# Cached keys of eight sampled rows: sixteen gather-and-attend steps taken two at a time, with six buffers of gathered rows in place of five

## The chip, the cores and the metric

The kernel runs on one core of a Trainium2 chip. The metric is the time of one execution on the device in microseconds (us). The engines are named as the profile names them: PE (matmul, with PEld for its weight loads), DVE, ACT, POOL and SP. DMAs are issued by SP or ACT, and, where the rows to fetch are looked up in a list of indices, by POOL.

## What is computed

One layer of a hybrid decoder for a prompt of 1024 rows and for eight sampled rows that each look back on 4096 cached rows. Only the sampled rows' attention over the cache is touched by the change:

```python
lat_past = cache_lat[page_table].reshape(Bd, -1, MLA_KV_RANK)      # 8 x 4096 x 128, gathered by pages
kr_past = cache_kr[page_table].reshape(Bd, -1, MLA_ROPE)           # 8 x 4096 x 32
q_lat = jnp.einsum('bshn,rhn->bshr', q_nope, w_uk)
s_past = jnp.einsum('bshr,btr->bhst', q_lat, lat_past) + jnp.einsum('bshp,btp->bhst', q_rope, kr_past)
s = jnp.concatenate([s_past, s_new], axis=-1) * MLA_SCALE
p = jax.nn.softmax(s, axis=-1)
o_lat = jnp.einsum('bhst,btr->bshr', p, lat_all)
```

Ahead of it stand the modulation, the input projection, the gated linear attention and the prompt's own attention; behind it the output projection and the layer norm of all rows.

## The kernel before

Each engine has its own program, written out by hand, and semaphores order them. The prompt's attention ends at about 560 us of the span. Then PE works through the cache in NSTEPS = 16 steps, two for each of the eight sampled rows. Step n handles 2048 cached rows: 128 partitions with 16 cached rows each, which is 128 x 2048 latent values and 128 x 512 rotary ones (1.3 MB).

For a step, PE does four things, and the rest of this text uses these letters for them:

- T(n): `keys_transposed(n, j)` for j = 0 to 3 (16 transposes of 128 x 128, L2403, into banks 0 to 3) and `rotary_transposed(n)` (4 more, L2410, bank 4). ACT copies each bank out (`keys_out`, L1267 and L1269). The key banks are single: a transpose of step n+1 into bank j waits until ACT has copied step n's bank j.
- S(n): `scores(n)`, 16 products over the latent keys (L2452) and 4 over the rotary ones (L2455), each f32 product being two instructions. They use 32 columns of the array each, so that four run beside each other.
- wT(n): `weights_transposed(n)`, one 128 x 128 transpose of the softmax weights (L2462).
- W(n): `weighted(n)`, 16 products with 32 columns each (L2471) that read the gathered rows themselves.

Between S and wT stand DVE's maximum (`largest`, L1758) and ACT's exponential (`weights`, L1277); between wT and W stands DVE's copy (`weights_out`, L1764); after W comes DVE's copy of the result (`values_out`, L1770). PE's order in loop round n is T(n+2), wT(n), S(n+1), W(n). ACT's is the five copies of step n+2, then the exponential of step n+1.

POOL issues the gathers (`gather(n)`, L872, L874, L875). There are UNITS = 5 buffers, and step n uses buffer n mod 5. A gather is two indirect DMAs, latent rows (L874) and rotary rows (L875). Buffer 2 lies in two pieces (slabs 1 and 2 of z), so its latent rows come in two DMAs (L872) and a gather into it is three. The first three gathers (2, 0, 1) are issued while the prompt's attention still runs; 3 and 4 wait for its last product; from 5 on, gather n waits for W(n-5) and for the maximum of step n-4.

The last two rounds carry extra work: PE's matmuls that spread the layer's gate over all rows (`gates_of_prompt`, `gates_of_samples`, L2476 and L2479), ACT's split of the output weights into a high part (`high_out`, L1281), eight pieces that go into buffers as they come free, and POOL's and ACT's split of the first prompt rows. Then DVE and PE merge the sixteen partial results (L1781 to L1807) between the first matmuls of the output projection (`high_rows`, L2495 and L2496). The gathered rows of steps whose buffers are slabs 1 and 2 and of the last ones must be read before ACT writes output weights over them.

## Time and profile before

| | us |
|---|---|
| runs shown (median of 3) | 745.33 |
| lowest, highest | 743.96, 746.56 |
| the profiled execution | 743.97 |
| its span in the trace | 742.1 |
| granted TensorE clock, mean | 0.995 of full |
| stretch from the first T in the loop to the first output matmul | 562.71 to 638.29 |

The span is the time from the first recorded instruction to the last; 1.9 us of the execution lie around it. A timeline row gives start, duration, engine, line, operation, output and input, shape, the count of merged instructions, and in brackets how long the engine was idle before it and what is taken to have ended the wait ("issue" means that the profile shows nothing that it waited for). Rows of PEld are the weight loads, and for f32 products they follow each other as the array takes them, so the start of one group to the start of the next is what the group costs PE. PE's own durations have the depth of the pipeline in them.

### The profile page before, as it was taken

How to read it: one execution, taken by the hardware profiler on the slowest of the kernel's cores; microseconds unless marked ns; L12 is line 12 of the kernel's file. 1: busy time of each engine (PE TensorE's matmuls, PEld its weight loads, DVE VectorE, ACT ScalarE, POOL GpSimd, SP SyncE). 2: the span in 40 equal slices, each digit the busy share in tenths (PEclk: the TensorE clock that was granted, in tenths of full speed). 3: DMA queues.
4: the chain of work that ended last, by engine and by line, in shares of the span. 5: the costliest groups of instructions: out<-in, count | busy, mean ns of one | idle time of the engine just before them, and what ended most of it. 6: DMA issues, size and time to landing. Idle time of an engine off the chain costs nothing.

```text
span 742.1 us, 16684 instructions
## 1 busy us (share of the span) xinstructions
PE 705.5 (95%) x7025; PEld 546.4 (74%) x7025; DVE 355.3 (48%) x782; ACT 327.3 (44%) x779; POOL 75.6 (10%) x113
## 2 busy tenths in 40 slices
PE   2799999999999999999999999999999999999995
PEld 1486878788789986777766666777677889678884
DVE  0454380030202025777675576667671111389977
ACT  1254651121212137667656566645675667602100
POOL 0000000000000010101111201132113443000000
PEclk9999999999999999999999999999999999999999
DMA  9995300303001011000010000202756774103332
GB/s 293 396 375 174 114 0 1 114 0 97 0 1 57 1 43 51 9 14 11 10 11 1 1 1 1 59 1 76 240 183 222 274 267 175 60 1 116 123 132 85
DMA packets 35301, 70.31 MB, mean 95 GB/s; under 512 B 6626, under 2 KB 17979, under 8 KB 33564
## 3 DMA queue, kind: packets, MB, share of 16 engines
q1 hardware_dynamic: 30602, 47.73, 19.8%
q0 software_dynamic: 4016, 20.97, 8.1%
q8 instruction: 56, 0.92, 0.5%
q10 hardware_dynamic: 610, 0.55, 0.3%
q14 instruction: 17, 0.14, 0.1%
HBM read 62.26 MB, written 6.07 MB: 92 GB/s over the span
## 4 chain that ended last, share of the span: by engine, by line
PE 90%; DVE 3%; SPq 2%; DMA 2%; ACT 1%; issue 1%; another core or an unknown queue 1%; DVEq 0%; ACTq 0%
PE banks L1988 21%; PE banks L2174 8%; PE banks L2000 6%; PE banks L2302 5%; PE banks L2383 4%; PE banks L2403 3%; PE banks L2152 3%; PE banks L2512 3%; PE banks L2514 3%; PE banks L2513 2%; PE banks L2090 2%; PE banks L2009 2%; PE banks L2452 2%; PE banks L2471 2%; PE banks L2495 2%; DMA s_x<-in_x_prompt 2%
## 5 line engine op out<-in xcount | busy, mean ns | idle before, releaser
L1044 ACT ACTIVATE s_z<-banks 128x512 f32<-128x512 f32 (+3 forms) x40 | 19.6, 501 | 130.0 <-PE banks L1988 130.0
L1988 PE MATMUL banks<-s_w_parts,s_h_b 128*128 128x272 f32 (+3 forms) x328 | 68.0, 323 | 0.0
L1253 ACT ACTIVATE s_z<-banks 128x512 f32<-128x512 f32 (+2 forms) x88 | 41.4, 517 | 47.1 <-PE banks L2383 46.3
L1417 DVE COPY s_zs<-banks 8x512 f32<-8x512 f32 (+3 forms) x6 | 3.5, 576 | 118.5 <-PE banks L1962 118.5
L1988 PEld LDWEIGHTS banks<-s_w_parts,s_h_b 128*128 128x128 f32 x328 | 49.3, 189 | 4.9 <-issue 1.7
L1244 ACT ACTIVATE s_z<-banks,s_temps 128x896 f32<-128x896 f32 (+7 forms) x64 | 47.2, 742 | 11.6 <-DVE s_temps L1712 8.6
L1988 PE MATMUL banks<-s_w_parts,s_h_a 128*128 128x256 f32 (+2 forms) x256 | 49.7, 314 | 0.0
L1988 PE MATMUL banks<-s_z_r,s_h_b 128*128 128x512 f32 (+1 forms) x152 | 48.8, 387 | 0.0
L2383 PEld LDWEIGHTS banks<-s_ident,s_z 128*128 128x128 f32 x288 | 33.3, 141 | 11.8 <-issue 5.5
L2383 PE MATMUL banks<-s_ident,s_z 128*128 128x128 f32 x288 | 39.8, 274 | 1.6 <-DVE s_z L1728 1.6
L1988 PE MATMUL banks<-s_z_r,s_h_a 128*128 128x512 f32 x128 | 40.9, 395 | 0.0
L1988 PEld LDWEIGHTS banks<-s_w_parts,s_h_a 128*128 128x128 f32 x256 | 36.0, 189 | 3.6 <-issue 0.4
L2302 PE MATMUL banks<-s_z 128*64 128x128 f32 x576 | 38.5, 278 | 0.0
L1267 ACT ACTIVATE s_z<-banks 128x512 f32<-128x512 f32 x64 | 33.1, 602 | 9.3 <-PE banks L2403 7.6
L2302 PEld LDWEIGHTS banks<-s_z 128*64 128x64 f32 x576 | 30.8, 136 | 5.4 <-issue 5.4
L1350 ACT ACTIVATE s_temps<-s_temps,s_eps_t 128x1 f32<-128x1 f32 (+1 forms) x9 | 2.6, 294 | 72.2 <-DVE s_temps L1845 72.2
L1728 DVE TENSOR_SCALAR s_z<-s_z,s_temps 128x896 f32<-128x896 f32 (+7 forms) x64 | 33.2, 540 | 1.7
L1712 DVE TENSOR_REDUCE s_temps<-banks 128x1 f32<-128x896 f32 (+3 forms) x32 | 32.8, 1024 | 1.1
L1988 PEld LDWEIGHTS banks<-s_z_r,s_h_b 128*128 128x128 f32 x152 | 28.5, 188 | 5.6
L1988 PEld LDWEIGHTS banks<-s_z_r,s_h_a 128*128 128x128 f32 x128 | 24.0, 188 | 6.7 <-issue 0.8
L2174 PE MATMUL banks<-s_kt,s_temps 96*128 96x512 f32 (+1 forms) x64 | 25.9, 527 | 0.0
L2174 PE MATMUL banks<-s_kt,s_z 96*128 96x512 f32 (+2 forms) x64 | 25.2, 515 | 0.0
(391 smaller groups left out, 1520.7 us busy)
## 6 DMA issues: line engine op xcount, KB each, us to landing
s_z<-in_w_ada SPq DMA_DIRECT2D x16, 512.0 KB, 12.2
s_temps<-in_w_in SPq DMA_DIRECT2D x3, 2048.0 KB, 7.7
s_x<-in_x_prompt SPq DMA_DIRECT2D x8, 512.0 KB, 11.8
s_z<-in_w_ada SPq DMA_DIRECT2D x1, 4096.0 KB, 13.8
s_kt<-in_w_out SPq DMA_DIRECT2D x8, 512.0 KB
s_temps<-in_x_prompt SPq DMA_DIRECT2D x8, 512.0 KB
out_y_prompt<-s_temps SPq DMA_DIRECT2D x7, 512.0 KB
s_temps<-in_w_in SPq DMA_DIRECT2D x2, 832.0 KB, 14.2
```

Source lines behind the costliest of these rows:

```text
L1244: last = nc.scalar.activation(weights_of(s, u), score_of(s, u), ACT.Exp, bias=nmx[:, c:c + 1], accum_out=rsum[:, c:c + 1])
L1253: nc.scalar.activation(PTb[r % 3][:, 4 * g:4 * g + n, :], banks[:, 4 + (groups(r) + g) % 2, 0:P * n].rearrange("p (j q) -> p j q", j=n), A ...
L1267: nc.scalar.activation(latT(n, j), banks[:, j, :], ACT.Copy).then_inc(f_Tc, 1)
L1712: nc.vector.tensor_reduce(nmx[:, c:c + 1], score_of(s, 0), AX_X, ALU.max, negate=True).then_inc(mx_ready, 1)
L1728: last = nc.vector.tensor_scalar(weights_of(s, u), weights_of(s, u), rinv[:, c + u:c + u + 1], None, ALU.mult)
L1988: last = nc.tensor.matmul(banks[:, proj_bank(c, t), 0:WIDTH[c]], h_[half][:, k, n0:n0 + P], w_, start=(k == 0 and n == 0), stop=(k == KT - ...
L2000: last = nc.tensor.matmul(banks[:, proj_bank(1, u), :], w_[:, k, P * m:P * m + P], h_[half][:, k, :], start=(k == 0 and n == 0), stop=(k = ...
L2152: last = nc.tensor.matmul(banks[:, q_bank(n, q), 0:384], z[:, BLOCKS[n], P * k:P * k + P], w_uq[:, k, 384 * q:384 * q + 384], start=(k == ...
L2174: last = nc.tensor.matmul(score_of(s, u)[:, n0:n1], QTb[n % 4][:, h, :], KTh[:, h, n0:n1], start=True, stop=True)
L2302: last = nc.tensor.matmul(banks[64 * par:64 * par + 64, 6, 0:P], V(j, 2 * hp + par), block, start=(j == 0), stop=(j == i))
L2383: last = nc.tensor.transpose(banks[:, 4 + k0 % 2, P * (b % 4):P * (b % 4) + P], Pm[r % 3][:, P * b:P * b + P], ident[:])
L2403: last = nc.tensor.transpose(banks[:, j, P * r:P * r + P], cached(n, 4 * j + r), ident[:])
```

## The change

- PE's loop goes over n = 0, 2, ..., 12 and does T(n+2), T(n+3), wT(n), wT(n+1), S(n+2), W(n), W(n+1), S(n+3). S(1) comes before the loop, next to S(0). The last two steps' wT and W stand behind the loop among the gate matmuls, all of which come after the last S.
- The scores of odd steps get a place of their own (bank 6, columns 256 to 383); both turned weights of a pair lie in bank 6; both results of a pair lie in bank 7, and DVE copies them out at once (128 x 256).
- ACT copies out ten banks (steps n and n+1) and then makes the weights of n and of n+1. DVE copies the two weights, then takes the maximum of n+2, copies the two results, and takes the maximum of n+3.
- wT(n) waits until the weights of both n and n+1 are there; W(n) of even n waits for DVE's copy of the last pair.
- Six buffers: the new one, buffer 3, is made of two query buffers of the prompt's attention (`qt1`, `qt3`, widened from 96 to 128 partitions). Buffers 2 and 3 are now the ones in two pieces, with three DMAs for a gather. Gather 3 is issued once the last scores of the prompt are done. Gathers 4 and 5 wait for the prompt's last product. From 6 on, gather n waits for W(n-6), and no longer for a maximum.
- ACT's high parts of the output weights go into the buffers in another order; the first is made before the weights of step 15 and all others after them. POOL's split waits for T(14).

```diff
-UNITS = 5
+UNITS = 6
+IN_HALVES = (2, 3)
...
-        w_out_hi = [slab_r(EARLY_SLABS[0]), slab_r(EARLY_SLABS[1]), slab_r(FIRST_KEYS[0]), slab_r(FIRST_KEYS[1]),
-                    z_rf[:, LAT3:LAT3 + D], z_rf[:, LAT3 + D:LAT3 + LAT], z_rf[:, LAT4:LAT4 + D], z_rf[:, LAT4 + D:LAT4 + LAT]]
+        w_out_hi = [z_rf[:, LAT3:LAT3 + D], z_rf[:, LAT3 + D:LAT3 + LAT], z_rf[:, LAT4:LAT4 + D], z_rf[:, LAT4 + D:LAT4 + LAT],
+                    slab_r(FIRST_KEYS[0]), slab_r(FIRST_KEYS[1]), slab_r(EARLY_SLABS[0]), slab_r(EARLY_SLABS[1])]
...
+        def scores_of(n):
+
+            return banks[:, 5, 0:P] if n % 2 == 0 else banks[:, 6, 256:256 + P]
...
+            pool.wait_ge(sc_done, len(STEPS))
+            gather(3)
             pool.wait_ge(pv_done, N_PAIRS_OF_HEADS)
-            for n in range(3, UNITS):
+            for n in range(4, UNITS):
                 gather(n)
             for n in range(UNITS, NSTEPS):
                 pool.wait_ge(f_o, n - UNITS + 1)
-                pool.wait_ge(f_mx, n - 3)
                 gather(n)
...
-            weights(0)
-            for n in range(NSTEPS):
-                if n + 2 < NSTEPS:
-                    for j in range(5):
-                        keys_out(n + 2, j)
-                if n + 1 < NSTEPS:
-                    weights(n + 1)
...
+            for n in range(2):
+                weights(n)
+            for n in range(2, NSTEPS, 2):
+                for j in range(5):
+                    keys_out(n, j)
+                for j in range(5):
+                    keys_out(n + 1, j)
+                weights(n)
+                if n == NSTEPS - 2:
+                    high_mixed(0)
                     act.wait_ge(w_out_in, 16 * KT)
...
+                    high_out(0)
+                weights(n + 1)
+            act.wait_ge(f_o, 12)
+            for k in range(1, 4):
+                high_out(k)
...
-            for n in range(NSTEPS):
+            for b in range(NB):
+                n = HALVES * b
                 weights_out(n)
-                if n + 1 < NSTEPS:
-                    largest(n + 1)
-                if n + 1 == NSTEPS:
+                weights_out(n + 1)
+                if b + 1 < NB:
+                    largest(n + 2)
+                else:
                     dve.wait_ge(f_mx, NSTEPS)
                     nc.vector.tensor_reduce(nmin, nm, AX_X, ALU.min).then_inc(f_dm, 1)
-                values_out(n)
+                values_out(b)
+                if b + 1 < NB:
+                    largest(n + 3)
...
             def weights_transposed(n):
-                pe.wait_ge(f_p, n + 1)
-                if n >= 1:
-                    pe.wait_ge(f_pTc, n)
-                nc.tensor.transpose(banks[:, 6, 0:P], p_s[n % 2], ident[:]).then_inc(f_pT, 1)
+                if n % 2 == 0:
+                    pe.wait_ge(f_p, n + 2)
+                    if n >= 2:
+                        pe.wait_ge(f_pTc, n)
+                nc.tensor.transpose(banks[:, 6, P * (n % 2):P * (n % 2) + P], p_s[n % 2], ident[:]).then_inc(f_pT, 1)
...
             scores(0)
-            for n in range(NSTEPS):
-                if n + 2 < NSTEPS:
-                    all_transposed(n + 2)
...
-                weights_transposed(n)
-                if n + 1 < NSTEPS:
-                    scores(n + 1)
...
-                weighted(n)
+            scores(1)
+            for n in range(0, NSTEPS - 2, 2):
+                all_transposed(n + 2)
+                all_transposed(n + 3)
+                weights_transposed(n)
+                weights_transposed(n + 1)
+                scores(n + 2)
+                weighted(n)
+                weighted(n + 1)
+                scores(n + 3)
+            pe.wait_ge(p_tabs, 16)
+            pe.wait_ge(f_Tc, 5 * NSTEPS)
+            gates_of_prompt(0)
+            gates_of_samples(0)
+            gates_of_prompt(1).then_inc(gate_b, 1)
+            weights_transposed(NSTEPS - 2)
+            weights_transposed(NSTEPS - 1)
+            gates_of_samples(1).then_inc(gate_b, 1)
+            pe.wait_ge(f_dm, MERGE["min"])
+            nc.tensor.transpose(banks[0:NB, 6, 256:256 + P], nmin, ident[:]).then_inc(p_pe, 1)
+            weighted(NSTEPS - 2)
+            weighted(NSTEPS - 1)
```

## Rows read from the trace of the kernel before

**Rows 1.** The page: busy time by engine, and the chain that ended last.

```profile
PE 705.5 (95%) x7025; PEld 546.4 (74%) x7025; DVE 355.3 (48%) x782; ACT 327.3 (44%) x779; POOL 75.6 (10%) x113
...
PE 90%; DVE 3%; SPq 2%; DMA 2%; ACT 1%; issue 1%; another core or an unknown queue 1%; DVEq 0%; ACTq 0%
```

**Rows 2.** Timeline of PEld, one round of the loop (n = 2).

```profile
573.51 1.73 PEld L2403 LDWEIGHTS banks<-s_ident,s_z 128*128 128x128 f32 x16 [0.20 <-issue]
575.21 0.47 PEld L2410 LDWEIGHTS banks<-s_ident,s_z 128*128 128x128 f32 x4
575.65 0.14 PEld L2462 LDWEIGHTS banks<-s_ident,s_z 128*128 128x128 f32 x1
575.95 0.81 PEld L2452 LDWEIGHTS banks<-s_z,s_temps 128*32 128x32 f32 x32 [0.17 <-issue]
...
576.96 0.89 PEld L2471 LDWEIGHTS banks<-s_z 128*32 128x32 f32 x32
578.06 0.20 PEld L2403 LDWEIGHTS banks<-s_ident,s_temps 128*128 128x128 f32 x2 [0.20 <-issue]
```

**Rows 3.** Timeline before the loop: 64-column products (L2302) between 128-column transposes.

```profile
552.63 0.42 PEld L2302 LDWEIGHTS banks<-s_z 128*64 128x64 f32 x8 [0.17 <-issue]
553.22 0.86 PEld L2383 LDWEIGHTS banks<-s_ident,s_z 128*128 128x128 f32 x8 [0.17 <-DVE s_z L1728]
554.05 0.91 PEld L2403 LDWEIGHTS banks<-s_ident,s_temps 128*128 128x128 f32 x8
```

**Rows 4.** Timeline of the first round: PEld, DVE and ACT.

```profile
562.27 0.24 PEld L2455 LDWEIGHTS banks<-s_z,s_temps 128*32 128x32 f32 x8
...
565.55 0.42 PEld L2410 LDWEIGHTS banks<-s_ident,s_w_uq 128*128 128x128 f32 x4 [0.85 <-issue]
...
565.77 0.29 DVE L1758 TENSOR_REDUCE s_temps<-banks 128x1 f32<-128x128 f32 x1 [5.81 <-remote]
...
568.97 0.14 PEld L2403 LDWEIGHTS banks<-s_ident,s_z 128*128 128x128 f32 x1 [0.20 <-issue]
```

**Rows 5.** Timeline of PEld, the round n = 3.

```profile
582.63 0.14 PEld L2455 LDWEIGHTS banks<-s_z,s_temps 128*32 128x32 f32 x2 [1.11 <-issue]
...
583.84 0.14 PEld L2403 LDWEIGHTS banks<-s_ident,s_temps 128*128 128x128 f32 x1 [0.20 <-issue]
```

**Rows 6.** Timeline of POOL: gather 2, gathers 3 and 4, gather 6, gather 7.

```profile
513.30 0.95 POOL L875 DMA_INDIRECT s_w_uq<-in_cache_k_rope,s_idx  x1 [0.30 <-issue]
...
559.91 0.95 POOL L874 DMA_INDIRECT s_z<-in_cache_kv_latent,s_idx  x1 [13.98 <-PE banks L2302]
...
563.66 0.95 POOL L875 DMA_INDIRECT s_z<-in_cache_k_rope,s_idx  x1 [0.30 <-issue]
...
573.89 0.94 POOL L874 DMA_INDIRECT s_temps<-in_cache_kv_latent,s_idx  x1 [2.35 <-PE banks L2471]
...
578.43 0.94 POOL L872 DMA_INDIRECT s_z<-in_cache_kv_latent,s_idx_half  x1 [2.35 <-PE banks L2471]
...
580.92 0.95 POOL L875 DMA_INDIRECT s_w_uq<-in_cache_k_rope,s_idx  x1 [0.30 <-issue]
```

**Rows 7.** Timeline of ACT: weights of step 3, first copies of step 5.

```profile
577.65 0.37 ACT L1277 ACTIVATE s_z<-banks,s_temps 128x128 f32<-128x128 f32 x1 [0.89 <-DVE s_temps L1758]
...
578.75 1.09 ACT L1267 ACTIVATE s_z<-banks 128x512 f32<-128x512 f32 x2 [0.65 <-PE banks L2403]
```

**Rows 8.** Stretches of 1 us: busy and count by engine, clock, DMA share, GB/s.

```profile
579.00:580.00 1.00, 1.00 (x12) 1.00 (x11) 0.00 (x0) 1.00 (x3) 0.70 (x2) 1.00 0.38 152
...
585.00:586.00 1.00, 1.00 (x12) 1.00 (x11) 0.00 (x0) 1.00 (x4) 0.69 (x2) 1.00 0.36 78
```

**Rows 9.** Timeline of PEld, behind the last full round.

```profile
630.53 0.30 PEld L2476 LDWEIGHTS banks<-s_modB,s_z 128*128 128x128 f32 x2 [0.20 <-issue]
...
634.78 0.22 PEld L2479 LDWEIGHTS banks<-s_modB,s_z 128*32 128x32 f32 x2
...
638.29 0.19 PEld L2495 LDWEIGHTS banks<-s_z_r,s_front_parts 128*128 128x128 f32 x1 [0.20 <-issue]
```

More of the change, by code:

```diff
@@ L281, in hybrid_step @@
         taken[0] = MLA_AT
[L282 to L283 removed]
+        qt1, qt3 = sb("qt1", [P, H * P]), sb("qt3", [P, H * P])
+        QTb = [v.rearrange("p (h s) -> p h s", h=H) for v in
+               (z[0:QK, 2, W_GV:W_GV + H * P], qt1[0:QK], carve(H * P, rows=QK), qt3[0:QK])]
         nmx = carve(8)
@@ L1276, in weights @@
                 b, c = divmod(n, HALVES)
-                nc.scalar.activation(p_s[n % 2], banks[:, 5, 0:P], ACT.Exp, bias=nm[:, b, c:c + 1],
+                nc.scalar.activation(p_s[n % 2], scores_of(n), ACT.Exp, bias=nm[:, b, c:c + 1],
                                      accum_out=o_all[:, b, c, KVR:KVR + 1]).then_inc(f_p, 1)
@@ L2470, in weighted @@
                         window = pTx[n % 2][:, g, :, :].rearrange("p r q -> p (r q)")[:, 32 * r:32 * r + 32]
-                        last = nc.tensor.matmul(banks[32 * g:32 * g + 32, 7, 0:KVR], window,
+                        last = nc.tensor.matmul(banks[32 * g:32 * g + 32, 7, KVR * (n % HALVES):KVR * (n % HALVES) + KVR], window,
                                                 cached(n, 4 * g + r), start=(r == 0), stop=(r == 3))
```

83 lines of the change are left out of this document (33 added, 50 removed).

## The prediction

> **What bounds the kernel now.** I read the page first. PE is busy 95% of the span and makes 90% of the chain that ended last [rows 1], so what counts is PE's own stream in the stretch that the change touches. That stretch is 562.71 to 638.29, 75.6 us. Next I read PEld's timeline, because the start of one group to the start of the next is what a group costs PE.
>
> One round takes 578.06 - 573.51 = 4.55 us [rows 2]. It divides into T 2.14 (573.51 to 575.65), wT 0.30, S 1.01 and W 1.10. The only idle times in it are 0.17 ahead of S and 0.20 ahead of the next T. Nobody releases them ("issue"), and they stand where the shape goes from 128*128 to 128*32 and back. Between wT and the T ahead of it, both 128*128, there is none; nor is there one between S and W, both 128*32, though W waits for two semaphores. Before the loop the same 0.17 stands ahead of 64-column products and behind them, and not between two kinds of 128-column transposes [rows 3]. I take the gap as the price of changing the shape of the weight tile.
>
> Three of the rounds are longer. The first takes 568.97 - 562.71 = 6.26: DVE gets its first scores at 565.77, three us after PE loaded the last weights of S(0), and PE itself is idle in pieces, the longest 0.85 [rows 4]. The round n = 3 takes 5.78, with a pause of 1.11 in the midst of S(4) [rows 5], and n = 8 repeats both. The other rounds from 1 to 13 take 4.55 each. POOL's rows show what is common: these two rounds hold the gathers into buffer 2, three DMAs in place of two, and the first round has four DMAs in one go, 559.91 to 564.61 [rows 6]. PE's pause ends 0.76 after the third issue ends (581.87), and each such round is longer by 1.24, which is one issue with its gap (0.94 + 0.30). I call this a hold. Its cause isn't in the trace. Gather 2, three DMAs ending at 514.25, met other PE work and no hold, so three issues alone don't make one [rows 6].
>
> **The change part by part.** The sum is made against the profiled execution, 743.97, which lies 1.36 under the median of the three runs, 745.33.
>
> *Order of PE's loop.* Nothing is removed from PE's work; two changes of shape in every two rounds go. A pair costs two T at 2.14 (4.28), the first wT 0.11 and the second 0.30, S 1.01, and W twice without its gap (1.10 - 0.22 = 0.88 each). The second S has ten turns of four matmuls at 0.11, thus 1.09, for it doesn't start on an empty array, and then 0.22 for the change back. Together 8.77 against 9.10 [rows 2]. Seven pairs save 7 x 0.33 = 2.3 us. Bounds: nothing, if the gap belongs to a wait after all, and 7 x 0.37 = 2.6.
>
> *Cover of ACT and DVE.* In the round before, ACT's weights begin 1.70 after S began (575.95 to 577.65) and its first copy 0.69 after T began [rows 2, 7]. In a pair the weights of n+1 end some 0.95 after T(n+2) began, so the ten copies start 0.26 later than a copy could. ACT makes a copy every 0.5 (two in 1.09), so bank 3 is free 3.0 after the pair began and bank 4, whose copy is a little longer, at 3.5; T(n+3) wants them at 3.45 and 3.84. It holds by 0.3. The copies of n+3 end at 6.1, S(n+3) wants them at 7.4. wT(n) now waits for two exponentials, the second of which is made at the start of the same pair, 3.3 early; behind it S and both W would queue. W(n) waits for DVE's copy, ready 5.1 after the pair began and wanted at 5.7. Cost 0; without that cover it would be 0.3 to 0.6 a pair.
>
> *Start.* S(1) ahead of the loop waits for ACT's copies of step 1, about 0.3. If the hold of f_sc stays until 565.7 [rows 4], ACT is the next to be late: it makes both first weights, to 567.2, before it copies T(2) out, and T(3) needs those banks. Copy by copy T(3) ends at 570.5, and the second pair begins at 574.9. Before, the third round began at 573.51, and with S(3) added 574.6. So this pair loses 0.3 where the sum above has it gain 0.33: +0.6. Bounds: 0 without the hold, +0.9.
>
> *Gathers.* The maximum that POOL waited for is long past before and goes without effect. From W(n)'s end to the start of pair n+4 are 10.4 us, for the second gather of a pair two more. POOL issues a pair of gathers in 4 or 6 DMAs of 1.24, thus 5.0 or 7.5, in a pair of 8.8, so it isn't the bound. A gather's data are through some 6 us after its first issue (573.89 to about 580), one of three DMAs after 7 to 8 (578.43 to about 586) [rows 6, 8]. For the pair 8 and 9 (and 14 and 15) the second is issued 3.7 after the first and is through at 11.7 against 12.6 allowed: free, by 0.9. Bounds: 0 and, if DMAs of both queue up, 1 to 2 us each.
>
> The Trainium skill ("DMA: Bandwidth & Descriptors", Bandwidth) would have transfers of at least 1 MiB and so speaks against pieces: by its fit (Anatomy of one DMA) a half costs an estimated 2.0 + 1.2 us, and six DMAs one after another about 18 us, which would make both pairs late by 5. The trace doesn't agree that the fixed parts add up: three DMAs were through after 8 us where this gives 9, and the DMA share falls to 0.36 only once all three are through.
>
> *Holds.* Before, two rounds pay 1.24. After, gathers 8, 9, 14 and 15 have three DMAs, but they go out as two runs of six, and all other gathers as runs of four. Part of each run falls on transposes. The fifth and sixth issue of a run of six end as S(n+4) begins, which is where the holds stood. I take two holds of 1.24, as before: 0. Bounds: -2.5 (none) and 1.7 to 2.5 for each of five runs, which is the excess of the first round and twice 1.24. Gather 3, moved ahead to 549.5, has three issues over 64-column products: between 0 (gather 2) and 1.24; I take 0, the row with the same three DMAs. On POOL nothing urgent is queued behind gather 3, and gathers 4 and 5 leave when 3 and 4 did.
>
> *End.* Before, 638.29 - 630.53 = 7.76 with S(15) in it, 6.7 without [rows 9]. After, the same matmuls stand there in another order, with two changes of shape fewer (0.4) but the minimum's transpose waits for both of DVE's copies behind wT(15), with only one gate matmul over them (0.4): 0, between -0.4 and +0.4. ACT's high parts end at 7.9 behind the last S and the merge wants ACT at 8.4, so this hides too; if it didn't, up to 1 us. DVE's copy of the last results is twice as wide and adds 0.1 to the merge. POOL's split of the first prompt rows stands behind its last gather, issued a pair and more before, and waits only for ACT.
>
> Sum: -2.3 + 0.3 + 0.6 + 0 + 0 + 0.1 = -1.3; with the start's wait for ACT's copies under the hold, -1.5. This gives 742.5 for the profiled execution and 743.8 from the median.
>
> **The rivals.**
>
> *The holds go away.* They stood where S met the third issue. If the new places (transposes under the third and fourth issue) have none, 2.5 more is gained, and if the first round's goes too, its excess of 1.7: 739.6 to 741.3, say 740.5. For it: gather 2. Against: the first round's reached into T(2) [rows 4].
>
> *A hold with every run of issues (slower than before).* All gathers go out in runs of four or six, and the only run of four before, at the start, cost 1.7 [rows 4, 6]. Three runs of four at 1.7 and two of six at 2.5, less the two old ones, is +7.6: 751.4. It decides from 0.3 us extra in each of the five runs on.
>
> *A late second gather or a late bank.* The margins are 0.9 for gathers 9 and 15 and 0.3 for ACT's copies. One or two of them missed cost 1 to 3: 745.3 to 747.
>
> *The change doesn't do what it says.* If the 0.17 and 0.20 belong to something in each step, the 2.3 stay away: about 746.
>
> **How the numbers follow.** A measurement of this kernel can tell about 0.3%, 2.2 us, from no change. Chances: my forecast (741.8 to 745.8 by its own bounds) 0.42, of which 0.15 gains over 2.2; holds gone 0.22, all faster; holds everywhere 0.14, all slower; late gather or bank 0.12, of which 0.09 slower; no effect 0.10, of which 0.02 slower. Faster 0.37, same 0.38, slower 0.25. The range reaches from the case with all holds gone, 739.5, to 748.5, in which a late gather and small holds are; the full price of holds everywhere stays out (0.14), and a little on the other side.
>
> **What will show it.** Right: pairs of 8.8 us in PEld's timeline, with one gap of 0.17 and one of 0.20 in each; "DMA" or ACT as releaser of T(9) or T(15) would show the third rival. A pause with "issue" inside S or T after the third or later indirect DMA shows holds; their number and place decide between the first two rivals. My start is right if DVE's first maximum comes near 565.7 and T(3) goes at ACT's pace. Wrong would be everything here if gaps of 0.17 stood inside W or between W and S.

## The result, and the profile after

The kernel after takes 771.0 us (median; 767.07 to 774.57), the kernel before beside it 745.9: ratio 1.034, interval 1.028 to 1.039. The forecast was 743.8 in a range of 739.5 to 748.5; range and sign were wrong.

The page of the kernel after: busy time, PE's busy share and TensorE's granted clock in 40 slices, and the chain that ended last.

```profile
PE 720.5 (94%) x7025; PEld 554.6 (72%) x7025; DVE 353.2 (46%) x774; ACT 326.1 (42%) x779; POOL 78.3 (10%) x116
...
PE   2799999999999989999999999999988788999996
...
PEclk9999999999999999999999999899999998999998
...
PE 90%; DVE 3%; issue 3%; ACT 1%; DMA 1%; ACTq 1%; another core or an unknown queue 0%; DVEq 0%
```

Busy times and chain look like [rows 1]. What points at the fault is small: "issue" at 3% in place of 1%, digits 8 and 7 in PE's row over the loop where the page before has 9 throughout, and three digits 8 in the clock. The same marks in both traces find it. From the start to the rotary DMA of gather 2 the profiled execution after is 3.71 longer (513.30 and 517.01), from there to the last transposes of step 1 another 1.66, over the scores ahead of the loop 3.77 (S(0) alone took 1.23, S(0) and S(1) take 5.00; some 1.1 of it is S(1), which the loop no longer has), from the first T of the loop to the first output matmul 18.57 (75.58 and 94.15), behind it -0.05. The sum is 27.66 = 771.63 - 743.97.

Stretches of the loop after: T(2) and T(3); S(2), W(0), W(1); S(3); then T(4) and T(5); later T(6) and T(7); T(12) and T(13); last a whole pair without gathers. Columns: stretch, its length, PE busy (operations), granted clock, DMA share, GB/s.

```profile
571.85:576.27 4.42, 4.42 (x41) 1.00 0.51 208
576.58:579.45 2.87, 2.87 (x106) 1.00 0.00 0
579.45:583.27 3.82, 2.52 (x48) 1.00 0.67 217
583.27:589.59 6.32, 6.12 (x41) 0.73 0.70 287
...
596.58:605.45 8.87, 6.79 (x40) 0.81 0.58 219
...
637.56:646.45 8.89, 7.48 (x41) 0.62 0.59 213
...
650.83:659.63 8.80, 8.80 (x190) 1.00 0.01 4
```

A pair that no gather disturbs takes 8.80 us; the forecast had 8.77. With a run of gathers, S of the odd step takes 3.8 to 4.0 in place of 1.21, and the transposes behind it 5.2 to 8.9 in place of 4.42. In three of these stretches TensorE's granted clock is below full (1.00 is 2.4 GHz, 0.50 is 1.2), behind the pauses of PE; (1 - clock) x length is 1.7, 1.7 and 3.4 us.

The timeline of one hold, after: POOL, PEld, DVE and ACT.

```profile
579.06 0.94 POOL L884 DMA_INDIRECT s_temps<-in_cache_kv_latent,s_idx  x1 [9.09 <-PE banks L2489]
580.30 0.95 POOL L885 DMA_INDIRECT s_temps<-in_cache_k_rope,s_idx  x1 [0.30 <-issue]
580.36 0.16 PEld L2469 LDWEIGHTS banks<-s_z,s_temps 128*32 128x32 f32 x5 [0.35 <-issue]
581.08 0.17 PEld L2469 LDWEIGHTS banks<-s_z,s_temps 128*32 128x32 f32 x5 [0.56 <-issue]
...
581.81 0.18 PEld L2472 LDWEIGHTS banks<-s_z,s_temps 128*32 128x32 f32 x5 [0.55 <-issue]
...
583.26 0.85 PEld L2418 LDWEIGHTS banks<-s_ident,s_z 128*128 128x128 f32 x6 [0.59 <-issue]
...
584.94 0.29 DVE L1768 TENSOR_REDUCE s_temps<-banks 128x1 f32<-128x128 f32 x1 [3.39 <-remote]
585.27 0.37 ACT L1288 ACTIVATE s_z<-banks,s_temps 128x128 f32<-128x128 f32 x1 [6.54 <-DVE s_temps L1768]
```

Two things start with the run of issues. PE stops when the first issue ends (580.00) and then gets through five or six weight loads and their products every 0.73 us, where an undisturbed S makes 40 weight loads in 1.1. And DVE's largest of step 3, whose scores end at 582.97, starts 1.97 later; ACT's exponential waits for it, and ACT's copies of T(4), which T(5) needs, stand behind the exponential. In this kernel that chain costs PE little: ahead of T(5) and its like PE stands 0 to 0.3 us, 0.7 in the five pairs together. The rest is PE's own slow pace and the clock: of the 12.7 us too much in the transposes 10.9 are in the first twenty of each pair (2.13 when undisturbed), where PE gets through four every 1.43 us while a run of six goes on:

```profile
597.99 0.42 PEld L2418 LDWEIGHTS banks<-s_ident,s_temps 128*128 128x128 f32 x4 [0.90 <-issue]
599.42 0.42 PEld L2418 LDWEIGHTS banks<-s_ident,s_temps 128*128 128x128 f32 x4 [1.01 <-issue]
```

Pauses of the first kind I call slow supply, late starts of the second kind late wake. Both stand in all five pairs with gathers. In the run of six, DVE's largest starts 4.76 after its scores end.

### The profile page after: what moved, and what is told of

Its sections match the earlier page's. It is cut to its first block, busy times and chain, and to the rows that moved or that the text cites. A ratio compares the mean times of both kernels' runs of the same rounds, so it can differ in the third digit from the quotient of the medians.

```text
span 769.8 us, 16643 instructions
## 1 busy us (share of the span) xinstructions
PE 720.5 (94%) x7025; PEld 554.6 (72%) x7025; DVE 353.2 (46%) x774; ACT 326.1 (42%) x779; POOL 78.3 (10%) x116
## 4 chain that ended last, share of the span: by engine, by line
PE 90%; DVE 3%; issue 3%; ACT 1%; DMA 1%; ACTq 1%; another core or an unknown queue 0%; DVEq 0%
PE banks L2003 20%; PE banks L2189 8%; PE banks L2015 6%; PE banks L2317 4%; PE banks L2418 4%; PE banks L2398 4%; PE banks L2167 3%; PE banks L2469 2%; PE banks L2530 2%; PE banks L2532 2%; PE banks L2531 2%; PE banks L2105 2%; PE banks L2024 2%; PE banks L2489 2%; PE banks L2513 2%
## 5 line engine op out<-in xcount | busy, mean ns | idle before, releaser
L1288 ACT ACTIVATE s_z<-banks,s_temps 128x128 f32<-128x128 f32 x16 | 5.9, 367 | 49.2 <-DVE s_temps L1768 49.0
```

## The experiments

In each group the kernels ran on one chip beside the kernel before. The span and the clock of every run come from a recorded execution; so nothing here tells what a run without recording would do. Edits are shown in part; "..." marks what is left out.

### On a chip where the kernel before takes 746.5 us

**a_no_gathers.** The loop of gathers n = 6 to 15 is left out, and PE's transposes wait only for a buffer's first gather.

```
-            for n in range(UNITS, NSTEPS):
-                pool.wait_ge(f_o, n - UNITS + 1)
-                gather(n)
...
-                pe.wait_ge(f_in[n % UNITS], (48 if n % UNITS in IN_HALVES else 32) * (n // UNITS + 1))
+                pe.wait_ge(f_in[n % UNITS], (48 if n % UNITS in IN_HALVES else 32))
```

> Changed kernel without the gathers of steps 6 to 15 (24 indirect DMAs of POOL); the last ten steps read the rows of steps 0 to 5 again, so the sample part of the output is not the reference's. Every theory has the holds come from these gathers, so the pairs should all take about 8.8 us like the two that have none running (T(14) at 650.83 to the gates at 659.63 in the changed kernel). The loop then lasts 7 x 8.8 = 61.6 us; in the changed kernel the stretch from T(2) (571.85) to the gates (659.63) is 87.8, so 26 us go: 771.0 - 26 = 745, and no fall of the granted clock inside the loop. If the pairs stay at 12 us or more, the gathers are not the cause and all three theories fall.

743.5 us, ratio 0.995 (0.994 to 0.997); two pairs of it, columns as above:

```profile
579.39:588.20 8.81, 8.81 (x191) 1.00 0.01 2
588.20:597.00 8.80, 8.80 (x191) 1.00 0.02 4
```

From the first T of the loop to the first output matmul it takes 67.99. The gathers of the loop thus cost 94.15 - 67.99 = 26.2 us in the kernel after: 13.5 in the five S of odd steps (over 1.21 each) and 12.7 in the five stretches of transposes behind them (over 4.42 each).

**a_small.** All 24 issues of the loop stay, with 128 bytes a row.

```
+                for out in outs + [kro[n % UNITS]]:
+                    nc.gpsimd.indirect_dma_start(out[:, 0:ROPE], None, one_rows, at).then_inc(f_in[n % UNITS], 16)
...
-                gather(n)
+                gather_small(n)
```

> Changed kernel in which every one of the 24 indirect DMAs of steps 6 to 15 is still issued by POOL at its place, over 128 rows, but moves 128 bytes a row (16 KB in place of 256 KB to 1 MB), so the sample part of the output is not the reference's. Theory issue (what slows PE is POOL's issuing: from the end of the first issue of a run to the end of the last, PE gets about 12 instructions in .72 us, 16 to 17 per us, while scores and values want some 80 per us and transposes 19): the holds and pair times stay as in the changed kernel, 765 to 771 us. Theory data (the gathered rows' traffic holds up PE's instructions or operands): holds shrink with the bytes, 745 to 748 us. Theory run length (three or more issues in a row hold PE, whatever runs on it): 765 to 771.

773.0 us, ratio 1.036 (1.033 to 1.040). The same pauses without the bytes; timeline, and the run of issues as one stretch (DMA share 0.06):

```profile
582.24 0.94 POOL L952 DMA_INDIRECT s_temps<-in_cache_k_rope,s_idx  x1 [0.30 <-issue]
...
583.00 0.17 PEld L2476 LDWEIGHTS banks<-s_z,s_temps 128*32 128x32 f32 x5 [0.56 <-issue]
...
583.74 0.18 PEld L2479 LDWEIGHTS banks<-s_z,s_temps 128*32 128x32 f32 x5 [0.56 <-issue]
```

```profile
580.98:585.98 5.00, 3.58 (x68) 1.00 0.06 13
```

Theory data falls: the traffic isn't the cause, the issuing is.

**b_under_S.** The kernel before, its two-DMA runs moved from beside the transposes to beside scores and values.

```
-                pool.wait_ge(f_mx, n - 3)
+                pool.wait_ge(f_T, 5 * (n - 1))
```

> Kernel before, with one wait changed: POOL's gathers of steps 5 to 15 start when all transposes of the round are done, not when they begin, so that the same two (in steps 7 and 12 three) issues of 1.24 us each lie beside the 32-column products of scores and values. Theory issue: about 74 instructions of PE in the 2.4 us of wT, S and W would be supplied at 16 to 17 per us while the issues last, so a round with two issues grows by some 1.7 us and one with three by 2.9: 9 x 1.7 + 2 x 2.9 = 21 us less the 2 holds of 1.24 that are there now, 764 us, more if the clock falls too. Theory run length: only the two runs of three hold PE, 745 to 747. Theory data: the traffic only moves by 2.1 us, 745 to 749 (the gather lands later by that much, still ahead of its transposes).

760.6 us, ratio 1.020 (1.017 to 1.022). Two issues, which beside T cost nothing in [rows 2], now stop PE in W:

```profile
573.72 0.94 POOL L874 DMA_INDIRECT s_temps<-in_cache_kv_latent,s_idx  x1 [7.51 <-PE banks L2410]
...
574.99 0.17 PEld L2471 LDWEIGHTS banks<-s_temps,s_z 128*32 128x32 f32 x6 [0.34 <-issue]
575.72 0.17 PEld L2471 LDWEIGHTS banks<-s_temps,s_z 128*32 128x32 f32 x5 [0.56 <-issue]
575.77 0.29 DVE L1758 TENSOR_REDUCE s_temps<-banks 128x1 f32<-128x128 f32 x1 [2.39 <-PE banks L2455]
```

Run length alone falls: a run of two is enough in the wrong place. The price a round (W 2.0 to 2.7 in place of 0.99, and behind some runs T 2.5 to 3.1 in place of 2.24) is near the 1.7 and 2.9 of theory issue, and so is the total, 760.6 where it had 764. DVE's largest is late in each of these rounds too, by 1.5 to 2.2.

**a_under_T.** The kernel after, both gathers of a pair behind the first transposes of the pair before.

```
+                pool.wait_ge(f_T, 5 * (n - n % 2 - 2) + 1)
```

> Changed kernel, with one wait changed: the gathers of steps n and n+1 (n even, 6 to 14) start when the first transposes of the pair before have been done, so that their four or six issues of 1.24 us begin beside transposes (4.3 us of them in a pair). Theory issue: transposes want 19 instructions per us and get 16 to 17, some .5 us a run; of a run of six (7.4 us) 2 to 3 us still reach into the scores and cost 1.7. Three runs x .5 + two x 2.2 = 6 us over a loop without holds (61.6 us against 87.8 in the changed kernel), so 771 - 26 + 6 = 751 us, and few or no falls of the clock. Theory run length: the holds stay as they are, about 770. Theory data: the rows move beside transposes and scores as before, 765 to 771, and the second gather of a pair may come late.

760.4 us, ratio 1.021 (1.015 to 1.026), where theory issue had 751: 10.6 of the 25 us come back from place alone, not 20. The transposes take 4.42 in every pair, beside up to 3.0 us of issuing. The rest is in the scores behind them, where the run isn't over: S 2.5 to 2.6 in place of 1.12 with 1.7 us of overlap, 5.2 with 4.1, and then the clock falls in the two long ones.

### On a chip where the kernel before takes 745.6 us

I now believed in a stock of instructions: place counts through what PE runs, and beside transposes all is well. That theory failed next.

**a_after_W.** Both gathers of a pair behind W of the odd step, 0.7 us ahead of the transposes.

```
-                pool.wait_ge(f_o, n - UNITS + 1)
+                pool.wait_ge(f_o, n - n % 2 - UNITS + 2)
```

> Changed kernel, with one wait changed: both gathers of a pair wait for the second products with the values (W of the odd step), so that a run of issues begins about .7 us ahead of the transposes, .9 us later than in the changed kernel. Four issues (4.97 us) then end before the 4.42 us of transposes do, six (7.45) reach about 2.0 us into the scores. Theory issue with a stock (PE has some 46 instructions in hand when a run of issues begins and gets 16 to 18 more per us while it lasts; transposes take 18.7 per us, scores and values about 80): the three runs of four cost nothing, the two of six 1.5 to 2 us each and perhaps a fall of the clock, so 743.5 (no gathers in the loop) + 4 = 747 to 749. Theory run length (any run of three or more costs): 758 to 770, at least what a_under_T measured (760.4), since nothing in the length of the runs has changed.

773.8 us, ratio 1.037 (1.033 to 1.042), against 747 to 749 expected. S of the odd step is at 1.21 again, with no stop in it. But DVE's largest of that step starts 2.7 to 3.4 after its scores, and the transposes take 7.6 to 11.1. So slow supply and late wake are separate, and the second costs as much.

**a_start.** Gather 5 behind S(0).

```
-            for n in range(4, UNITS):
-                gather(n)
+            gather(4)
+            pool.wait_ge(f_sc, 1)
+            gather(5)
```

> Changed kernel, with the gather of step 5 taken out of the run of four issues beside S(0) and S(1) (565.28 to 570.25, where S(0) and S(1) take 5.0 us in place of 2.4) and put behind S(0), beside the transposes of steps 2 and 3. Theory issue with a stock: the hold of 2.5 us ahead of the loop goes and none comes in its place, 771.0 - 2.5 = 768.5. If what holds PE there is the first scores themselves (their waits, their first operands), S(0) and S(1) stay at 5.0 us and the time at 771.

767.6 us, ratio 1.029 (1.026 to 1.033). S(0) and S(1) take 2.4 in place of 5.0, as expected. But something did come in its place: gather 5 is issued from 564.90 on, 0.85 ahead of the end of S(1), DVE's largest is 2.03 late, PE stands 1.4 for ACT's copies, and T(2) and T(3) take 5.90 in place of 4.42. The time agrees with the 768.5 expected all the same, and in part by luck: the fall of the clock near 484 us, of which more below, is not in this trace.

**a_direct.** Plain DMAs from POOL with the same bytes, at the same places.

```
+                    nc.gpsimd.dma_start(lat[n % UNITS], lat_rows[P * n:P * n + P, :]).then_inc(f_in[n % UNITS], 16)
+                nc.gpsimd.dma_start(kro[n % UNITS], kro_rows[P * n:P * n + P, :]).then_inc(f_in[n % UNITS], 16)
...
-                gather(n)
+                copy_rows(n)
```

> Changed kernel in which the 24 DMAs of steps 6 to 15 are still started by POOL at the same places, with the same bytes and shapes of destination, but as plain DMAs from consecutive rows, not as indirect ones, so the sample part of the output is not the reference's. If it is the indirect issue (rows' addresses worked out on POOL, .94 us each) that holds PE, no hold and no fall of the clock in the loop, 743 to 745 us. If any DMA that POOL starts does it, or the traffic of these rows does, 760 to 771.

745.2 us, in one run. The scores end, DVE starts at once, and PE goes on, at a DMA share of 0.95 (two stops of another kind, 1.59 and 0.82, are left; the last section has them):

```profile
576.13 0.57 POOL L952 DMA_DIRECT2D s_temps<-in_cache_kv_latent  x1 [8.98 <-PE banks L2497]
...
577.83 0.29 DVE L1776 TENSOR_REDUCE s_temps<-banks 128x1 f32<-128x128 f32 x1 [0.67 <-PE banks L2480]
```

```profile
577.79:583.00 5.21, 5.21 (x63) 1.00 0.95 376
```

**a_spread.** Rotary gathers dealt out ahead, so that a run has four issues (twice five), all runs from W of the odd step, gather 5 behind S(0).

```
...
+            for n, ahead in ((6, (8, 9)), (8, ()), (10, (10, 11, 12)), (12, (13, 14, 15)), (14, ())):
+                pool.wait_ge(f_o, n - 4)
+                gather_latent(n)
+                gather_latent(n + 1)
+                for k in ahead:
+                    gather_rotary(k)
```

> Changed kernel with all gathers but two placed by the theory issue with a stock: the rotary rows, whose buffers come free one or more pairs earlier than the latent rows', are issued ahead (those of step 3 behind gather 1, the others so that a run in the loop has four issues, twice five), each run begins at the end of W of the odd step, .7 us ahead of the transposes, and gather 5 stands behind S(0). The pairs are then 8.8 us each with at most .5 us more where there are five; the stretch ahead of the loop loses the 2.5 us of S(0) and S(1) and the 1.7 us of the pause behind gather 3. 743.5 - 2.5 - 1.7 + 1 = 740.3 us, against 746.5 for the kernel before. Theory run length: all runs of four and five hold PE still, 755 to 765. If gathers come late for being issued later, pairs of 9 to 10 us and 744 to 750.

771.7 us, ratio 1.035 (1.031 to 1.039), a miss by 31 us: with late wake in each of six runs the transposes take 7.6 to 10.0. The part ahead of the loop did what was expected (S(0) and S(1) 2.4, the pause behind gather 3 gone from 1.8 to 0.4).

### On a chip where the kernel before takes 741.7 us

**a_spread_act.** a_spread with ACT's exponential of the odd step behind the copies of the next even one.

```
                 for j in range(5):
                     keys_out(n, j)
+                weights(n - 1)
                 for j in range(5):
                     keys_out(n + 1, j)
```

> a_spread with one edit on ACT alone: the exponential of an odd step (L1288 of the changed kernel), which needs DVE's largest of that step, stands behind the five copies of the next even step's transposes, not ahead of them. In a_spread DVE's largest of the odd step starts 2.7 to 4.9 us after its scores end, when a run of issues is on; ACT's exponential waits for it, the copies behind that wait, and the transposes of the second step of the pair wait for the copies. Theory chain (DVE is held by the issues, and PE stands in the transposes only for it): the transposes of a pair fall from 7.6 to 10.0 us to 4.4 to 5, six times, so 771.7 - 28.7 + 3 = 746 us. Theory PE (the issues hold PE itself, whatever ACT and DVE do): the transposes stay above 6 us, 760 to 772.

**a_spread_S.** a_spread with runs that also wait for the scores of the odd step; gather 5 waits for S(1), not S(0).

```
                 pool.wait_ge(f_o, n - 4)
+                pool.wait_ge(f_sc, n - 2)
```

> a_spread with one edit on POOL alone: a run of issues waits for the scores of the odd step as well (f_sc), so that it begins about .8 us behind the start of the transposes, after DVE's largest and ACT's exponential of that step have begun, not .7 us ahead of it. Theory chain plus stock: DVE and ACT are through before the issues begin and the transposes take 4.4 us; four issues then reach .9 us, five 2.1 us into the scores, where PE has a stock of 46 instructions and 16 to 18 more per us: .2 and 1.8 us of hold. 743.5 - 2.5 - 1.7 + 4 x .2 + 2 x 1.8 = 743.7 us. Theory run length: 770 still. Theory position against scores alone (as I held before a_spread): worse than a_spread by the .9 us more in the scores, 775.

**a_best.** a_spread_S with the rotary gathers dealt out evenly: (6: 9, 10), (8: none), (10: 11, 12), (12: 13, 14), (14: 15), those of 6 and 8 ahead of the loop, and each waiting for the transposes that free its buffer.

> a_spread_S with the rotary rows dealt out evenly, so that five of the six runs in the loop have four issues and the last has five. By theory chain plus stock 743.5 - 2.5 - 1.7 + 5 x .2 + 1.8 = 742.1 us, against 746 for the kernel before; the gain over a_spread_S is one hold of 1.6 us. If it is not below 745, the pair order has no gain left once its gathers are paid for.

742.1, 745.5 and 743.3 us, ratios 1.001 (0.998 to 1.004), 1.005 (1.002 to 1.007) and 1.003 (1.001 to 1.006). I read the first as proof of the chain DVE, ACT, PE. It was none: the chip was another one, and the kernel before had shown it by being 4 us faster than elsewhere. That is about what its own holds cost (1.7 + 2 x 1.24, [rows 4, 5]); that they are what is missing isn't shown, since there is no trace of it from this chip.

### On a chip where the kernel before takes 746.6 us

**a_act** is the kernel after with the edit on ACT; **a_after_W_act** is a_after_W with it; **a_spread_act_small** is a_spread_act with 128 bytes a row.

> The changed kernel itself with the edit on ACT alone: the exponential of an odd step stands behind the five copies of the next even step's transposes. In the changed kernel the five scores of odd steps beside a run of issues take 13.4 us more than their 1.21, and the five pairs of transposes behind them 12.7 us more than their 4.42. If the second part is the chain DVE, ACT, PE and the fall of the clock that the waiting brings, it goes for the greater part and the first stays: 771.0 - 10 = 761 us. If the issues hold PE in the transposes by themselves, 770.

> Changed kernel with the two one-line edits that do nothing or little alone: the gathers of a pair behind W of the odd step (a_after_W, 773.8 us against 771.0) and the exponential of the odd step behind the copies of the even one. Both causes out of the way together: runs of four beside transposes cost nothing, runs of six reach 2 us into the scores and cost 1.5 each, the stretch ahead of the loop keeps its 4.2 us, and one or two stops of 1.5 to 2.5 us at a block of PE's instructions as in a_spread_act: 743.5 + 3 + 3 = 749 to 750 where the kernel before has 746. If the two causes simply add and each is small, 765 to 770.

> a_spread_act in which the DMAs of the loop (issued at their places) move 128 bytes a row, so the sample part of the output is not the reference's. In a_spread_act PE stops three times (.3, 2.5 and 1.7 us) at instructions whose number is 193 more than a multiple of 256, each time with a 16 KB fetch of queue q8 that starts 60 to 250 instructions later than in the kernel without gathers. If the gathers' bytes hold up the fetch, the fetches come on time (190 to 250 behind the multiple), the three stops go and the time is 742.1 - 4.5 = 737.6 us. If POOL's issuing holds it up, 742.

774.3, 775.9 and 774.9 us, ratios 1.036, 1.038 and 1.037 (all intervals above 1.031): the edit on ACT gives nothing, and neither the 761 nor the 749 to 750 expected came. In the kernel after there was little to gain, since PE stands for ACT's copies for 0.7 us in all. The third run leaves its question open: on this chip PE stops for the issues with 128 bytes too, and the three stops stand neither in its trace nor in that of a_spread_act_again, with all bytes. In a_after_W, where PE stands 2.1 to 2.8 us for ACT in each pair, the edit could have gained. The trace of a_after_W_act shows why it didn't. ACT's next operation is now a copy whose input T(4) gave at 579.20, and it too starts only when the run is over:

```profile
577.83 0.94 POOL L884 DMA_INDIRECT s_temps<-in_cache_kv_latent,s_idx  x1 [11.74 <-PE banks L2489]
578.54 1.73 PEld L2418 LDWEIGHTS banks<-s_ident,s_z 128*128 128x128 f32 x16 [0.20 <-issue]
...
581.56 0.95 POOL L885 DMA_INDIRECT s_temps<-in_cache_k_rope,s_idx  x1 [0.30 <-issue]
582.16 0.29 DVE L1768 TENSOR_REDUCE s_temps<-banks 128x1 f32<-128x128 f32 x1 [4.14 <-remote]
583.61 2.07 ACT L1278 ACTIVATE s_z<-banks 128x512 f32<-128x512 f32 x4 [6.98 <-remote]
584.32 2.63 PEld L2418 LDWEIGHTS banks<-s_ident,s_z 128*128 128x128 f32 x16 [3.61 <-issue]
```

DVE and ACT both come to a wait for PE in the run, and start 3.5 and 4.4 us after their input is there. Late wake isn't DVE's alone.

**b_spread.** The kernel before with its gathers placed by this account.

```
+            pool.wait_ge(f_T, 7)
+            gather_rotary(5)
             pool.wait_ge(pv_done, N_PAIRS_OF_HEADS)
-            for n in range(3, UNITS):
-                gather(n)
+            gather(3)
+            pool.wait_ge(f_sc, 1)
+            gather(4)
@@
-                gather(n)
+                gather_latent(n)
+                if n != 7:
+                    gather_rotary({5: 6, 6: 7}.get(n, n))
```

> The kernel before with its gathers placed by what the runs showed and nothing else changed: one rotary gather ahead of the last products with the values, gather 4 behind the first scores in place of a run of four beside them, the rotary rows of steps 6 and 7 one round early, so that step 7's round has two issues, not three. The round of step 0 loses its 1.7 us (transposes 2.24 in place of 3.9), one of the two holds of 1.1 goes: 2.8 us faster than the kernel before, ratio 0.996. If length and place of the runs don't matter in this order, no difference.

742.7 us against 746.6, ratio 0.995 (0.993 to 0.998): 3.9 us faster, a little more than the 2.8 worked out, and ahead of both kernels. The first T of the loop, which had DVE 2.96 late and PE at 3.90 us, is undisturbed (564.34 to 566.47), and one hold of the two is left, at step 12:

```profile
564.34 1.73 PEld L2415 LDWEIGHTS banks<-s_ident,s_z 128*128 128x128 f32 x16 [0.20 <-issue]
564.69 0.29 DVE L1770 TENSOR_REDUCE s_temps<-banks 128x1 f32<-128x128 f32 x1 [3.10 <-PE banks L2467]
...
566.47 0.14 PEld L2474 LDWEIGHTS banks<-s_ident,s_z 128*128 128x128 f32 x1
```

### On a chip where the kernel before takes 746.1 us

**a_spread_act_again** and **a_best_again** repeat these two kernels. **a_busy** is a_direct with a clear of the buffer ahead of each DMA.

```
+                nc.gpsimd.memset(out, 0.0).then_inc(f_clear, 1)
+                pool.wait_ge(f_clear, cleared[0])
```

> The kernel of a_spread_act once more, on another chip. It gave 742.1 us on a chip where the kernel before gave 741.7, a_spread 771.7 and a_spread_act_small 774.9 on chips where it gave 745.6 and 746.6. Theory chip (what a run of issues costs depends on the chip, the order of ACT does nothing): where the kernel before needs 745 to 747, 768 to 775 us with DVE's largest late by 2.5 to 5 us and transposes of 7 to 10 us. Theory chain (the order of ACT is what helped, and only the bytes made it fail in a_spread_act_small, little as that would make sense): 742 to 747 there too.

> The kernel of a_best once more, on another chip (it gave 743.3 where the kernel before gave 741.7): pair order, runs of four issues (once five) that begin after the scores of the odd step, in time beside the transposes. Where the kernel before needs 745 to 747 by the holds, theory issue: DVE's largest is through before the issues begin, so the transposes stay at 4.42 us, and four issues reach .9 us into the scores, which in a_under_T cost 1.3 with 1.7 us of overlap: .5 to 1.3 each, 743.5 - 4.2 + 5 to 9 = 744 to 748 us. If place doesn't decide on such a chip: 760 or more.

> a_direct (plain DMAs of consecutive rows in place of the indirect ones, so the sample part of the output is not the reference's; 745.2 us) with POOL kept busy at the same places: ahead of each DMA it clears 900 columns of the buffer (512 for the rotary rows), some .9 and .5 us by its rows of a 640-column clear in .65 us. If any work of POOL beside DVE's and PE's holds these, 760 us or more, with DVE's largest late. If it must be the indirect issue, 745 to 747.

a_spread_act_again takes 773.6 us, ratio 1.037 (1.033 to 1.041), where the same kernel took 742.1. The same place in both traces, first on the chip of 741.7, then here: in both, S(1) ends 0.85 after the run's first issue began.

```profile
563.29 0.94 POOL L884 DMA_INDIRECT s_z<-in_cache_kv_latent,s_idx  x1 [0.98 <-PE banks L2487]
...
564.18 0.29 DVE L1783 TENSOR_REDUCE s_temps<-banks 128x1 f32<-128x128 f32 x1 [0.77 <-PE banks L2487]
...
564.74 2.06 ACT L1293 ACTIVATE s_z<-banks 128x512 f32<-128x512 f32 x4 [0.83 <-PE banks L2433]
```

```profile
567.04 0.94 POOL L884 DMA_INDIRECT s_z<-in_cache_kv_latent,s_idx  x1 [1.09 <-PE banks L2487]
...
572.80 0.29 DVE L1783 TENSOR_REDUCE s_temps<-banks 128x1 f32<-128x128 f32 x1 [5.64 <-remote]
572.86 2.06 ACT L1293 ACTIVATE s_z<-banks 128x512 f32<-128x512 f32 x4 [5.20 <-remote]
573.57 3.03 PEld L2433 LDWEIGHTS banks<-s_ident,s_qt 128*128 128x128 f32 x16 [3.62 <-issue]
```

DVE is 0.04 late on the one, 4.91 on the other. So the order on ACT wasn't what helped, and what a run of issues costs goes with the chip, or with where in it the core lies, or with something else that differed between the two sittings; no run tells these apart. One of the five chips on which these experiments ran had none of it, in three kernels.

a_best_again takes 748.7 us, ratio 1.003 (1.001 to 1.005). Its runs of issues start after DVE and ACT have begun, beside the transposes, and reach 1.1 us into the scores:

```profile
580.20 1.78 PEld L2439 LDWEIGHTS banks<-s_ident,s_z 128*128 128x128 f32 x16
...
582.80 0.59 PEld L2490 LDWEIGHTS banks<-s_z,s_temps 128*32 128x32 f32 x24 [0.17 <-issue]
583.93 0.11 PEld L2490 LDWEIGHTS banks<-s_z,s_temps 128*32 128x32 f32 x1 [0.54 <-issue]
584.65 0.23 PEld L2490 LDWEIGHTS banks<-s_z,s_temps 128*32 128x32 f32 x7 [0.61 <-issue]
```

All stretches of transposes take 4.42; S of the even step takes 2.33 in place of 1.12 four times, 1.95 once and 3.70 once, where the run has five. Against a_spread, which issues nearly the same DMAs 1.5 us earlier relative to the transposes, this is 23 us.

a_busy takes 748.0 us in its one run, with no operation of DVE late (the fall of the clock near 484 us is in this trace, not in that of a_direct):

```profile
580.86 0.55 POOL L952 MEMSET s_temps<- 128x512 f32 x1
581.09 0.29 DVE L1787 TENSOR_REDUCE s_temps<-banks 128x1 f32<-128x128 f32 x1 [0.67 <-PE banks L2491]
```

Neither POOL's other work nor the bytes, then, but the issue of an indirect DMA. For a_direct and a_busy this rests on one run each, and on their traces, in which no engine starts late.

## Why the prediction was wrong

*Order of PE's loop:* right. A pair takes 8.80 (8.77 forecast), with one gap of 0.17 and one of 0.20. From S(0) to the first output matmul a_no_gathers takes 72.84, before 76.81. These 4.0 are the 2.3 of the order and the 4.2 that the old holds and the first round cost, less 2.5 at the start.

*Cover of ACT and DVE:* right for undisturbed pairs only, which have no idle time of PE. I had checked that ACT keeps pace with PE, and not that ACT's exponential, ahead of ten copies, can make PE wait for DVE once DVE is late: 0.7 us in all in the kernel after, 2.1 to 2.8 a pair in a_after_W.

*Start:* the number came out by luck, the path was wrong. In a_no_gathers, which keeps the gathers ahead of the loop, the stretch from S(0) to T(4) takes 13.65; before, with 1.1 for S(3) added, 13.1. The 0.5 fits the +0.6 and +0.3 less 0.33. But T(3) doesn't go at ACT's pace: T(2) and T(3) take their 4.42 in both kernels. In its place the run of four lay beside S(0) and S(1), which take 5.00 in the kernel after, 2.6 more than the 2.4 of a_start; PE stood, and DVE's lateness lay hidden beside it. After:

```profile
570.89 0.43 PEld L2469 LDWEIGHTS banks<-s_z,s_temps 128*32 128x32 f32 x16 [1.26 <-issue]
...
571.85 1.73 PEld L2418 LDWEIGHTS banks<-s_ident,s_z 128*128 128x128 f32 x16 [0.20 <-issue]
```

*Gathers' data:* right. PE waits for no DMA in the loop after. The rows of the first run of six are through 10.4 us after its first issue begins (592.37 to 602.77), where I had 11.7. The rule of the Trainium skill that I weighed ("DMA: Bandwidth & Descriptors", Bandwidth) had nothing to do with the loss: with 1/64 of the latent bytes it stays (a_small). Nor do the 2.0 us of its fit add up over six DMAs issued behind each other, as the estimate of 18 us had them.

*Gather 3:* taken at 0, measured 1.66; PE's pause behind its three issues is 1.79.

*End:* 6.37 from the last S to the output matmuls, 6.7 less up to 0.4 in the forecast: right.

*Holds:* here the prediction failed, in the term "I take two holds of 1.24, as before: 0". It was 26.2 less the two old ones, +23.7. The rival "a hold with every run of issues" named the right mechanism and place, and had 0.14; it too was far off, since it priced five runs at 1.7 to 2.5, from the first round and twice the hold of before, and they cost 3.6 to 7.3 each. Three things in that price were wrong. I took the number of issues as the cause, and it was what lies beside them: two cost nothing beside transposes and 1.0 to 1.7 beside 32-column products (b_under_S). [rows 2, 6] show it, had I asked how much of a run lies beside which work: all runs in the loop before begin 0.4 into T, 2.14 long, and only those of three reach well into S. The change moved the issues from T to W and S. Then the late start of DVE in the first round [rows 4] stood in my rows as "the hold of f_sc" and I costed it once, at the start, not as something that comes with every run. And the fall of TensorE's clock behind long pauses, up to 6.8 us by the three stretches above, wasn't in the sum.

*The 3.71 ahead of 517* go with the granted clock, which is at 0.50 for 6.8 us there, some 3.4 of the 3.71. PE is busy throughout.

```profile
486.00:490.00 4.00, 4.00 (x37) 0.50 0.00 0
```

What lowered it is open. It isn't of this execution alone: such a fall, beginning between 482 and 486 us, stands in 11 of the 17 traces of the kernel after and its variants, a_no_gathers among them, and in none of the three of before, b_under_S and b_spread. So it is not the gathers of the loop; whether it belongs to the change isn't shown, since three traces are few, and PE's matmuls there are the same. It does not make the verdict: a_no_gathers has the kernel's own order, buffers and loop ahead, and the fall too, and is 3.0 faster than the kernel before.

**What stays open.** Why issuing an indirect DMA keeps PE at some 16 instructions per us, and keeps a waiting engine from starting, isn't shown. The steps of 0.7 us are common to both (DVE late by 1.30, 1.97, 2.70, 3.38, 4.07 and 4.76 in after, a_small and a_after_W; PE's period 0.73), so I take it for one cause in what feeds the engines' instructions or signals. I didn't settle it. The Trainium skill ("NOTIFIC — the notification-queue block", 7.1 Overflow) says that the block that records instructions can hold up an engine when its own pipeline is full; PE's pace under the issues would suit such a limit, and no run here shows it, since all are recorded. The kernel after itself was not run on the chip without holds.

## What to carry to other kernels

Before you move a wait of the engine that issues gathers, write down what every other engine does in the next 5 us: issues that were free beside a few long operations cost from half their length up to all of it beside many short ones (b_under_S, a_under_T), or when they start while another engine stands waiting (a_after_W). Start them when the others are busy with long operations, keep the runs short, and send the pieces whose buffers come free early ahead of the rest (b_spread: 0.5% from place alone). And when two kernels ran on different chips, compare each with its own run of the reference kernel before you believe in the edit: here the same kernel differed by 31 us between two chips, and the kernel before by 4.

## What I had not expected of the hardware

- One indirect DMA takes POOL 0.94 us and 0.30 to the next, with 128 bytes a row (a_small) as with 8 KB. A plain one takes 0.57, and no engine starts late beside it (a_direct).
- On four of five chips, while such issues run, PE gets through 11 to 12 instructions every 0.73 us from the end of the first issue on, where its products are short. Transposes, at 19 instructions per us, go on at 4.42 a pair if the run starts after them (a_under_T, a_best_again); those that begin 4 us into a run of six come four every 1.43 us (the kernel after). Overlap of a run with wT, scores or values of up to 0.4 us cost nothing, 1.1 us cost 1.2, 1.7 cost 1.2 to 1.6; 4.2 cost 4.1 where the run was long under way (a_under_T) and 2.6 to 2.8 where it had only begun (the kernel after).
- There, an engine that comes to a wait in a run starts 1.3 to 4.9 us late. ACT, going from copy to copy, keeps up with PE, but stops for 0.85 once or twice a run though its input has been there for 0.5 us and more (a_best_again).
- A third kind of stop appeared once these were out of the way. In a_best, 1.3 to 1.7 us each:

```profile
590.37 0.25 PEld L2490 LDWEIGHTS banks<-s_z,s_temps 128*32 128x32 f32 x9 [1.41 <-issue]
```

Numbering PE's recorded instructions, such stops stand at 10945, 11713 and 12481, three blocks of 256 apart, and the queue q8 moves 16 KB for each block. In the kernel without gathers that transfer begins 198 to 236 instructions behind a block's start, in a_best up to 399; a_direct, with the bytes and without the indirect issues, has it at 404 and stops of 1.59 and 0.82 at the same numbers. So the late block goes with the rows' traffic, and doesn't need indirect issues. That short work beside each other uses up 256 instructions sooner in pair order (S, W, W, S in one piece) is my reading and not tested.
